# Gates of the first tile of tokens added into DRAM element by element, instead of built from one-hots

## The reference, cut to what matters

```
q = xt @ w_pq                                # 8 heads
s1, s2 = q[..., :half] @ keys1.T, q[..., half:] @ keys2.T   # 128 scores each
v1, i1 = top_k(s1, 16);  v2, i2 = top_k(s2, 16)
sc, ci = top_k(v1[:, None] + v2[None, :], 16)
eid  = i1[ci // 16] * 128 + i2[ci % 16]      # 8 heads x 16 = 128 experts for each token
gate = softmax(sc)
hid  = gelu(x . expert_u[eid])
out  = sum(gate * hid * expert_v[eid])
```

## Time and profile before

| | |
|---|---|
| time, median of 3 runs | 2102.1 us |
| the profiled execution's own time | 2104.66 us |
| its span | 2102.9 us |
| PE (TensorE) | 2014.8 us, 96% |
| PEld (weight loads) | 1848.3 us, 88% |
| DVE (VectorE) | 1619.8 us, 77% |
| ACT (ScalarE) | 793.6 us, 38% |
| POOL (GpSimd) | 543.4 us, 26% |
| mean granted TensorE clock | 0.979 of full speed |
| DMA | 483.75 MB, mean 230 GB/s |

### The profile page before, as it was taken

The page is one execution under the profiler, slowest core; times in us unless marked ns, Lnnn a source line. Parts: engine busy times, 40 slices in busy tenths (PEclk is TensorE's granted clock), DMA queues, the critical chain, the costliest instruction groups (busy, mean ns, idle before and its releaser), DMA issues.

```text
span 2102.9 us, 33945 instructions
## 1 busy us (share of the span) xinstructions
PE 2014.8 (96%) x12943; PEld 1848.3 (88%) x12943; DVE 1619.8 (77%) x3030; ACT 793.6 (38%) x1311; POOL 543.4 (26%) x334
## 2 busy tenths in 40 slices
PE   8998889889999899999999999999989999999998
PEld 8998879768866899999999999999978888888886
DVE  6635766565254325999999799999969999999997
ACT  4335453442241322332344344444434333333332
POOL 0000020000000000112111045555537656666530
PEclk9999889999999999999999999999999999999999
DMA  5223210061451402677676579999999999999982
GB/s 172 85 98 117 81 52 1 23 224 41 177 193 54 161 1 97 223 271 253 221 246 241 182 240 333 330 333 331 336 377 388 411 412 411 411 412 411 408 353 92
DMA packets 205520, 483.75 MB, mean 230 GB/s; under 512 B 11983, under 2 KB 104655, under 8 KB 205286
## 3 DMA queue, kind: packets, MB, share of 16 engines
q1 hardware_dynamic: 159334, 314.56, 41.3%
q0 software_dynamic: 46080, 167.79, 21.6%
HBM read 423.29 MB, written 58.36 MB: 229 GB/s over the span
## 4 chain that ended last, share of the span: by engine, by line
PE 57%; DMA 2%; SPq 1%; ACT 0%; DVE 0%; issue 0%; POOL 0%; ACTq 0%; DVEq 0%
PE ps L3000 24%; PE ps L2608 8%; PE ps L2604 8%; PE ps L2603 8%; PE ps L2594 5%; PE ps L2632 3%; DMA experts<-peer_u 1%; DMA outputs<-peer_v,kept 1%; SPq L2585 1%; SPq L2563 0%; ACT scores L2689 0%; DMA hidden<-kept 0%; PE ps L3026 0%; ACT kept L2678 0%; SPq L2552 0%
## 5 line engine op out<-in xcount | busy, mean ns | idle before, releaser
L3000 PE MATMUL ps<-v_high_low,gated_high_low 128*128 128x512 f32 x2304 | 526.1, 390 | 9.2 <-ACT gated_high_low L3068 7.5
L3000 PEld LDWEIGHTS ps<-v_high_low,gated_high_low 128*128 128x128 f32 x2304 | 434.0, 188 | 101.1 <-ACT v_high_low L3066 7.8
L2603 PE MATMUL ps<-x_high_low,u_high_low 128*128 128x384 f32 x1024 | 355.6, 347 | 0.2 <-ACT u_high_low L2669 0.2
L2604 PE MATMUL ps<-x_high_low,u_high_low 128*128 128x384 f32 x1024 | 345.0, 337 | 0.0
L3092 POOL DMA_INDIRECT outputs<-peer_v,kept x138 | 258.3, 1871 | 154.9 <-DVE kept L3109 118.3
L2720 POOL DMA_INDIRECT scores<-peer_u,kept x64 | 94.1, 1470 | 733.7 <-DVE kept L2840 556.8
L2678 ACT ACTIVATE kept<-ps 128x384 f32<-128x384 f32 x128 | 62.9, 491 | 405.8 <-PE ps L2608 402.6
L2608 PE MATMUL ps<-x_high_low,u_high_low 128*128 128x384 f32 x1024 | 204.7, 341 | 0.0
L2603 PEld LDWEIGHTS ps<-x_high_low,u_high_low 128*128 128x128 f32 x1024 | 192.5, 188 | 0.5 <-ACT u_high_low L2669 0.5
L2604 PEld LDWEIGHTS ps<-x_high_low,u_high_low 128*128 128x128 f32 x1024 | 192.8, 188 | 0.0
L3109 DVE SCALAR_TENSOR_TENSOR kept<-outputs,kept 128x1024 f32<-128x1024 f32 x136 | 174.2, 1281 | 8.4 <-DMA outputs<-peer_v,kept 4.7
(11 more groups left out here) (471 smaller groups left out, 4123.5 us busy)
## 6 DMA issues: line engine op xcount, KB each, us to landing
experts<-peer_u SPq DMA_DIRECT2D x63, 1024.0 KB
raw_v<-peer_v SPq DMA_DIRECT2D x60, 1024.0 KB
hidden<-kept SPq DMA_DIRECT2D x64, 384.0 KB
gates<-scores SPq DMA_DIRECT2D x12, 2048.0 KB
first_hidden<-hidden SPq DMA_DIRECT2D x16, 768.0 KB, 10.2
outputs<-gates SPq DMA_DIRECT2D x16, 768.0 KB
outputs<-hidden SPq DMA_DIRECT2D x16, 768.0 KB
first_gates<-gates SPq DMA_DIRECT2D x15, 768.0 KB
```

The lines of the kernel that those rows point to most:

```text
L2603: pe.matmul(o, utr[:, b, HI, k], xr[:, HI, k, 0:DN], start=(k == 0), stop=False)
L2604: pe.matmul(o, utr[:, b, HI, k], xr[:, LO, k, 0:DN], start=False, stop=False)
L3000: ins = pe.matmul(bank(c, 2 * t + h), gr[:, slot, x, DN * b + P * t:DN * b + P * t + P], vr[:, slot, y, D * b + 512 * h:D * b + 512 * h + ...
```

## The change

Only tiles 1 and 2 go through the one-hots. The gates of tile 0 are added into a table in DRAM that was zeroed in the delta phase: one DMA for each of the 128 picks, of 128 elements of 4 bytes (one for each token), with its addresses from a tile of indices. GpSimd issues them; between two heads (16 adds) it waits until those issued have landed, since two heads of a token can have picked the same pair. Among the 16 adds of a head it issues 20 row gathers.

Tile 0 is picked first, then tile 4 in a quarter of the work (two heads in each group of 32 partitions), then 3, 1, 2. Token groups are 8 instead of 12, so 94 blocks come without tokens and 32 with. The group's store goes from SyncE to ScalarE. 122 of the 160 dot products are done ahead of the tokens, where there were 59, and the planner's numbers are others.

```diff
 phase_delta
+    zeros, zeros_set = words(c, A_XT, 8, 4 * P), s("zeros_set")
+            sp.wait_ge(zeros_set, 1)
+            for q in range(0, NK // 4, 8):
+                sp.dma_start(gate_quads(c)[:, q:q + 8, 0:4].rearrange("p q g x -> p q (g x)"), zeros).then_inc(c.gates_zeroed, 16)
             sp.wait_ge(uw, NT)
+            pool.memset(zeros, 0.0).then_inc(zeros_set, 1)
 phase_hidden
-BEFORE = NQ - QT * NTG - 1
+ADDED = P // TG
+NOH = NTG - ADDED
+DO = NOH * TG
+BEFORE = NQ - QT * NOH - 1
-GATES_AT = 25
-DOT_EVERY, LOW_EVERY = 2.2, 4.7
-DOTS_BY = {4: 0, GT: 16, 0: 32, 1: 46, 2: 59}
+PICKS = (0, 4, GT, 1, 2)
+EXPS_AT = {0: 5, GT: 19}
+DOT_EVERY, LOW_EVERY = 1.9, 4.9
+DOTS_BY = {0: 0, 4: 0, GT: 28, 1: 56, 2: 84}
+BEFORE_GATES = 122
+FETCHED_FIRST, FETCHED_BETWEEN = 5, 20
 SyncE
             def first_values(j):
                 if j == 1:
                     sp.wait_ge(gates_set, 1)
+                    sp.wait_ge(gkept, (NOH - 1) * QG)
 ...
                 if j == 2:
 ...
+                    sp.wait_ge(added, 16 * PAIRS)
                     sp.dma_start(hid_first, hidden_blocks(c)[:, 0:4]).then_inc(c.first_gated, 16)
 ...
+            sp.wait_ge(gates_stored[1], 16 * (NOH // 2))
 TensorE
-            for n in range(DENSE):
-                if n >= 2:
-                    pe.wait_ge(pairs_out, n - 1)
+            for n in range(2):
                 for i in range(3):
-                    ins = pe.transpose(bank(c, 6 + n % 2)[:, P * i:P * i + P], kept[:, n, i], ident)
+                    ins = pe.transpose(bank(c, 6 + n)[:, P * i:P * i + P], kept[:, n + 1, i], ident)
 ScalarE
+            def store_gates(tg, slot):
+                act.wait_ge(gkept, tg * QG + QG)
+                act.dma_start(gate_quads(c)[:, :, bass.ds(tg + ADDED, 1)].rearrange("p q g x -> p q (g x)"),
+                              gst[slot].rearrange("p (q b) t -> p q (b t)", b=4)).then_inc(gates_stored[slot], 16)
+            span(act, 3, EXPS_AT[0], both)
+            exps_set(0)
+            span(act, EXPS_AT[0], EXPS_AT[GT], both)
+            exps_set(4)
+            exps_set(GT)
 GpSimd
+            def add_gate(i):
+                pool.indirect_dma_start(out=all_gates, out_offset=bass.IndirectOffsetOnAxis(ap=spot[:, i:i + 1], axis=0),
+                                        in_=gates_of[0][:, i:i + 1], in_offset=None, compute_op=ALU.add).then_inc(added, 16)
+            no = 0
+            while no < FETCHED_FIRST:
+                fetch(no)
+                no += 1
+            pool.wait_ge(spots_set, 1)
+            for i in range(PAIRS):
+                if i and i % TOPK == 0:
+                    pool.wait_ge(added, 16 * i)
+                add_gate(i)
+                while no < min(ROWSETS, FETCHED_FIRST + FETCHED_BETWEEN * (i + 1) // TOPK):
+                    fetch(no)
+                    no += 1
 VectorE
                     if dots[0] < upto:
                         dot()
-                        spent[0] += 1.3
+                        spent[0] += 1.75
+            def place_first():
+                divided(0)
+                key, quad = kept[:, 0, 0], spot
+                step(v.tensor_copy(quad, key))
 ...
+                v.tensor_copy(spot, at_row).then_inc(spots_set, 1)
+            more, start = UG * BEFORE - lows[0], dots[0]
+            for i in range(more):
                 low()
+                while dots[0] < start + (BEFORE_GATES - start) * (i + 1) // more:
+                    dot()
+            divided(4)
+            divided(GT)
             v.wait_ge(sums, 1)
-            step(v.reciprocal(inv, bank(c, 6, DN)))
+            step(v.reciprocal(inv, bank(c, 6, DO)))
-            for o in range(NTG * QG // 2):
+            for o in range(NOH * QG // 2):
```

More of the change, by code:

```diff
@@ L2693, in _, with exps_set @@
                 both(q, q % 2)
[L2694 to L2698, removed]
+            def exps_set(n):
+                act.wait_ge(picked, order[n] + 1)
+                act.activation(gates_of[n], kept[:, n, 2, 0:pairs_of(n)], ACT.Exp).then_inc(exp_s, 1)
+            span(act, 3, EXPS_AT[0], both)
[3 more added lines that the diff above has]
+            exps_set(GT)
+            span(act, EXPS_AT[GT], BEFORE - 2, both)
             both(BEFORE - 2, 1)
[L2701 removed]
+            for n in range(2):
                 act.wait_ge(pairs_turned, n + 1)
[L2703 to L2704 removed]
+                act.copy(kt[:, 0:3, P * n:P * n + P], bank(c, 6 + n, 3 * P).rearrange("p (i t) -> p i t", i=3)).then_inc(pairs_out, 1)
+            act.wait_ge(pairs_out, 2)
             act.activation(gate, kt[:, 2], ACT.Exp).then_inc(exps, 1)
@@ L2725, in _ @@
             step = c.dve_step.on(v)
-            lows, dots, spent = [0], [0], [0.0, 0.0]
+            lows, dots, spent, due = [0], [0], [0.0, 0.0], []
             def low():
@@ L2787, in pick @@
-                step(v.tensor_tensor(c3[:, :, 9], b2[:, 0, :, 8:16], b2[:, 1, :, 0:1].broadcast_to([P, PH, 8]), ALU.add))
-                between(1.8, upto)
-                t3, p3 = (x.rearrange("p (h k) -> p h k", h=PH) for x in (top, pair))
-                best16(lambda g: cand[:, g], lambda g: t3[:, g], lambda g: p3[:, g], PH, 0.3, upto)
+                r, heads = pairs_of(n), pairs_of(n) // TOPK
+                part = r / PAIRS
+                top, pair, hi, lo, hif, lof = (row[0][:, 0:r], *(x[:, 0:r].bitcast(U32) for x in row[1:4]), row[4][:, 0:r], row[5][:, 0:r])
@@ new lines, in pick @@
+                v.tensor_tensor(few[:, :, 0:16], b2[:, 0, :, 0:1].broadcast_to([P, heads, 16]), b2[:, 1], ALU.add)
+                v.tensor_tensor(c3[:, :, 2:9], over(b2[:, 0, :, 1:8], 3, [P, heads, 7, 8]), over(b2[:, 1, :, 0:8], 2, [P, heads, 7, 8]), ALU.add)
+                step(v.tensor_tensor(c3[:, :, 9], b2[:, 0, :, 8:16], b2[:, 1, :, 0:1].broadcast_to([P, heads, 8]), ALU.add))
+                between(1.8 * part, upto)
+                t3, p3 = (x.rearrange("p (h k) -> p h k", k=TOPK) for x in (top, pair))
@@ L2791, in pick @@
+                best16(lambda g: cand[:, g], lambda g: t3[:, g], lambda g: p3[:, g], heads, 0.3, upto)
                 v.tensor_scalar(hi, pair, 3, None, ALU.logical_shift_right)
                 step(v.tensor_scalar(lo, pair, 7, None, ALU.bitwise_and))
-                between(0.8, upto)
-                v.tensor_tensor(kept[:, n, 2].rearrange("p (h k) -> p h k", h=PH), t3, over(t3[:, :, 0], 2, [P, PH, 16]), ALU.subtract)
+                between(0.8 * part, upto)
+                v.tensor_tensor(kept[:, n, 2, 0:r].rearrange("p (h k) -> p h k", k=TOPK), t3, over(t3[:, :, 0], 2, [P, heads, 16]), ALU.subtract)
@@ L2825, in pick @@
-                return v.tensor_tensor(kept[:, n, 0:2].rearrange("p s r -> p (s r)"), tree[:, :, 0], tree[:, :, 1], ALU.add)
-            def divided(n, i):
-                v.wait_ge(exp_s, i + 1)
-                g3 = gates_of[n].rearrange("p (h k) -> p h k", h=PH)
-                step(v.tensor_reduce(head_sum, g3, AX, ALU.add))
-                step(v.reciprocal(head_sum, head_sum))
-                return v.tensor_tensor(g3, g3, over(head_sum, 2, [P, PH, TOPK]), ALU.mult)
-            pick(4, DOTS_BY[4]).then_inc(picked, 1)
@@ L2836, in _ @@
-            v.wait_ge(picked, 1)
-            step(v.scalar_tensor_tensor(eid, kept[:, 4, 0], float(NK), kept[:, 4, 1], ALU.mult, ALU.add))
-            for i in range(QUADS):
-                r = slice(SAMP * i, SAMP * i + SAMP)
-                ins = v.tensor_copy(ids[r, 0:PAIRS_EACH], eid[r, PAIRS_EACH * i:PAIRS_EACH * i + PAIRS_EACH])
-            ins.then_inc(ids_set, 1)
-            v.wait_ge(xs_in, 16 * QUADS)
-            pick(GT, DOTS_BY[GT]).then_inc(picked, 1)
-            v.wait_ge(picked, 2)
@@ L2845, in _ @@
-            step(v.scalar_tensor_tensor(tail, kept[:, GT, 0], float(NK), kept[:, GT, 1], ALU.mult, ALU.add))
-            v.tensor_copy(ids[:, PAIRS_EACH:], tail).then_inc(ids_set, 1)
-            for n in range(3):
-                pick(n, DOTS_BY[n]).then_inc(picked, 1)
-                v.wait_ge(picked, n + 3)
-                if n == 1:
-                    while lows[0] < UG * GATES_AT + 1 and lows[0] < UG * BEFORE - 1:
-                        low()
-                    step(divided(4, 0))
-                    step(divided(GT, 1))
@@ L2855, in _, with expert_ids @@
-            while lows[0] < UG * BEFORE:
+                    between(cost * part, upto)
+                v.tensor_tensor(kept[:, n, 0:2, 0:r], spots[:, :, :, 0], spots[:, :, :, 1], ALU.add).then_inc(picked, 1)
+                v.wait_ge(picked, order[n] + 1)
+            def expert_ids(n, cols):
+                at = at_row[:, 0:pairs_of(n)]
+                step(v.scalar_tensor_tensor(at, kept[:, n, 0, 0:pairs_of(n)], float(NK), kept[:, n, 1, 0:pairs_of(n)], ALU.mult, ALU.add))
+                v.tensor_copy(ids[:, cols], at).then_inc(ids_set, 1)
```

154 lines of the change are left out of this document (100 added, 54 removed).

## The result

The changed kernel takes 2119.3 us (median of 4 runs) beside 2101.5 for the kernel before: 1.0088 times as long, 95% interval 1.0073 to 1.0104. I had forecast 2091. The profiled execution took 2113.9 (span 2112.1), 9.2 more than the one of before (2104.7). Stage by stage: the hidden stage (first transposes to the end of the last third pass) took 1560.1 - 809.4 = 750.7 us, against 740.2 before; the gap ahead of combine 12.4 against 7.5; combine 539.6 against 540.3; all that lies ahead of the hidden stage 5.4 us less (whether by the change or by chance is left open, see the last run). 10.5 + 4.9 - 0.7 - 5.4 = 9.3.

A forecast was written before the change was run, and what follows sets the result against it. TensorE was taken as the bound, with VectorE also full in blocks with tokens. Terms -28.7 - 0.8 + 1.5 + 12.6 + 2.7 + 2 = -10.7 us took the median from 2102.1 to 2091, range 2075 to 2119.

The forecast's parts named there:

- Rival C: GpSimd's issue of an add takes twice a gather's, 1.9 us, so the kernel takes 2120 us; chance 0.22.
- deciding point: Price of an add's issue, 1.35 us (0.41 above a gather), from which the kernel is not faster.
- Token groups and turned pairs: Hidden stage: 16 blocks lose their tokens, 28.7 us less; 9 transposes become 6, 0.8 us less.
- Zeroing: Delta phase: four DMAs of 2 MB while DMA engines are idle; taken as 0, bounds 0 and 3 us.
- Start: Start of the hidden phase: late copy and first dot's row wait cost 1.5 us more, bounds 0 and 5.
- Picks, no loss: Picks with more dots: VectorE's 97.5 us of work fits in 106.5 and GpSimd's 62 us fits; no cost.
- my sign of being wrong: The forecast is wrong if TensorE waits in the picks already, or the gap before combine exceeds 20 us.
- Last 16 blocks: Before the tokens, TensorE waits for `low` behind dots waiting for rows: 12.6 us more, bounds 0 and 56.
- Handover: To the tokens: three dots and two divisions stand before the first octet's reciprocal, 2.7 us more, bounds 0 and 5.4.
- End: Before combine: SyncE's wait for adds delays its first loads, so the gap grows 2 us, bounds 0 and 12.

The follow-up runs named there:

- the last run: The kernel before, unchanged, traced a second time; its hidden stage began at 817.5 us, against 814.8 in its first trace.
- e3: The changed kernel with the same 128 scatters written plainly, without the sum: 2103.3 us.
- e7: The changed kernel with no dot before the 16th lower half, 104 dots before the tokens for 122, 18 gathers between adds for 20: 2075.4 us.
- e9: e7 without its 128 adds and without SyncE's wait for them: 2077.1 us.
- e4: The changed kernel with no dot placed before the 16th lower half: 2108.4 us.
- e1: The changed kernel without the 128 adds and SyncE's wait for them: 2081.2 us.
- e8: The changed kernel with 14 gathers instead of 20 among a head's 16 adds: 2143.3 us.

## Why the prediction was wrong

The step that failed is the sentence "I take an add's issue as a gather's, since both make addresses for 128 rows". The issue takes 1.585 us at the least instead of 0.94, and 1.89 on the mean where it mattered. What the sentence says of addresses was nearly right (0.989 without the sum); it left out the sum, the one thing that no row of before showed. Rival C had this mechanism, its price (1.9) and its result (2120) to a microsecond, and its deciding point, 1.35 us an add, lies below every add of the trace. I gave it 0.22 because I argued from the addresses alone, and let the range end at 2119, short of C's own 2120. Of the 28 us between 2091 and 2119 the sum in the adds is 16 (e3). That 2120 and 2119 agree so well is partly luck: C had 1.5 us for the start of the stage, which cost 11.9, and did not have the earlier start (-5.4); the two partly cancel.

Point by point:

- *Token groups and turned pairs, -29.5.* Right. With the stalls gone the hidden stage takes 1521.0 - 807.4 = 713.6 us (e7) and 713.5 (e9), against 740.2: 26.6 less, where the terms with the start's 1.5 say 28.0 less. The pitches are again 5.073 and 6.87 (1397.17 to 1438.38 in the kernel after, six blocks).
- *Zeroing, 0.* Right: four issues on SyncE, 14 us in all, and in the kernel after nothing ahead of the hidden stage became later.
- *Start, +1.5.* Wrong: 11.9 us, beyond its bound of 5. From the start of the stage to the third pass of block 16 it took 98.2 us in the kernel after, 86.3 before and 89.9 in e4, so 8.3 are the first dot's and 3.7 are left for the rest, inside the bounds. I took over a wait of 2.42 us "without loss to TensorE" and did not ask which `low` is behind the dot. After a quarter pick the planner's counter lets a dot come in front of a due `low`; the first row took 5.5 us from the end of its issue (886.48 to 892.00), not 3.3, and by my own sum TensorE can stand a `low` only 3.9 us late.
- *Picks, no loss.* Right from 900 to 1200 us, where TensorE is busy without a gap. But my sign of being wrong, a wait of TensorE in the picks, did show: 8.7 of its 23.6 us of waits for `low` stand before 900 us, in the first picks, and 6.5 of these are the first dot's.
- *Last 16 blocks, +12.6.* The place and the way (rows late, dots late, `low` late) were right, the size wrong, by the price of an add: with plain writes (e3) the hidden stage is 740.3 - 722.9 = 17.4 us longer than in e1, against the 12.6 + 2.7 of my sum for this part and the handover. The hidden stage of after is 750.7 - 722.9 = 27.8 us longer than that of e1, all of it here and at the handover. Between 1230 and 1350 us TensorE is busy 99.3 us in after and 117.9 in e1: 18.7 us are idle time. The other 9 fit the slow clock behind the waits, which no term of mine had: granted 0.91 over these 120 us against 1.00 in e1, so some 21 us at the lower level, which loses half of them, about 10 by this estimate. The stretch of issues beside VectorE is there too: gathers 1.05 to 1.11 instead of 0.94, adds 1.89 instead of 1.585. (Two small slips in that part: 97.6 less 81.2 and 3.9 is 12.5, and the ends of the dot and the one-hot that I gave are the starts of what follows them; by the rows they end 0.07 to 0.08 us later.) The Trainium skill's page "SBUF — State Buffer", section "Who interferes with whom", would have had none of it; these rows, like those of before, speak against that inference.
- *Handover, +2.7.* 5.8 us, just above its bound, but not a cost of its own: with 104 dots it was 1.0.
- *End, +2.* 4.9. The order was as I said (SyncE held by the adds), yet what ended the gap was ScalarE's last store, which I had only as traffic. By e7 and e9 a gap of 10 us can come without late adds.
- With an add at a gather's price the forecast would have held but for the start: plain scatters gave 2103, and 8 less for the first dot would be 2095. This sum was not run as one kernel.

## What to carry to other kernels

Before new DMAs go into an engine's queue, find a row for that very kind of issue, its sum included; where there is none, the chance belongs to the side whose deciding point is closest, here 0.41 us. When a wait moves in front of other work, ask what is due behind it, not how long it was before. And where one queue serves two clients, its order can matter more than its load: the same 288 issues gave 2143, 2119 and, with 18 dots moved, the first ones held and 18 gathers between for 20, 2075 us.

## What the runs showed of the hardware

- An indirect DMA from GpSimd that adds 128 elements of 4 bytes into DRAM takes 1.585 us to issue at the least (kernel after; 1.557 to 1.586 in the eight kernels with adds), without the sum 0.989 (e3), a gather of 128 rows of 4 KB 0.933.
- The means over the hidden stage, mostly beside work of VectorE, are 1.98 (after), 1.43 (e3) and 1.17 to 1.25 (after).
- In the kernel before, the 100 gathers whose first 0.94 us overlap an instruction of VectorE with two operands in SBUF take 1.78 us on the mean, the 41 that overlap of the long ones only a `low`, with one operand in PSUM, 0.94.
- From the issue of the last gates' store (2 MB) to the next stage's first work it took 10.7 us where 2 MB had been asked for 7 us earlier (e1, e8), 16.2 where it was 3 us earlier (e7, and e9 with 16.1), 18 with 3.4 MB in the 4 us before (after).
- Behind a wait of TensorE of 5 us the next third pass took 2.93 us instead of 1.67, with a granted clock of 0.57 in the 4 us around it.
